# Norm of the latents issued under the last gate tile, with the latent attention's buffers laid out anew

## What is computed

```python
z = h @ w_in
qa, ka, va, cq, ckv, kpe, gate = jnp.split(z, ATT_SPLITS, axis=-1)
cq = _rmsnorm(cq, g_qa)
q_nope = jnp.einsum('bsc,chd->bshd', cq, w_uq)
q_pe = _rope(jnp.einsum('bsc,chr->bshr', cq, w_uqr), pos)
q_lat = jnp.einsum('bshd,chd->bshc', q_nope, w_uk)
ckv = _rmsnorm(ckv, g_kva)
kpe = _rope(kpe[:, :, None, :], pos)[:, :, 0, :]
# differential attention on qa, ka, va; latent attention on q_lat, q_pe, ckv, kpe
o = jnp.concatenate([o_a, o_b], axis=-1) * jax.nn.silu(gate)
return o @ w_out, new_rows
```

## Time and profile before

| | us |
|---|---|
| median of 3 runs | 2079.89 (2076.95 to 2081.9) |
| profiled execution | 2074.99 |
| its span | 2073.2 |
| TensorE busy | 1850.0 (89%) |
| VectorE busy | 1255.5 (61%) |
| ScalarE busy | 411.3 (20%) |
| GpSimd busy | 197.4 (10%) |
| mean granted TensorE clock | 0.945 |

### The profile page before, as it was taken

The page is one execution under the profiler, slowest core; times in us unless marked ns, Lnnn a source line. Parts: engine busy times, 40 slices in busy tenths (PEclk is TensorE's granted clock), DMA queues, the critical chain, the costliest instruction groups (busy, mean ns, idle before and its releaser), DMA issues.

```text
span 2073.2 us, 32711 instructions
## 1 busy us (share of the span) xinstructions
PE 1850.0 (89%) x13182; PEld 1699.9 (82%) x13182; DVE 1255.5 (61%) x1598; ACT 411.3 (20%) x912; POOL 197.4 (10%) x117
## 2 busy tenths in 40 slices
PE   5548999999999978997987899968999999999995
PEld 0108999999999966776876778957999999999995
DVE  4899667667867653554355544376777544584444
ACT  1241000000010012332355443431000000131111
POOL 2770000000600000000000011210000000001110
PEclk8879999999999999998889898989999999999997
DMA  9555555545655422216134244214444333452222
GB/s 388 226 223 192 205 191 212 193 189 193 238 205 209 182 102 62 62 32 178 60 113 138 84 143 173 91 61 158 180 182 187 126 108 120 163 194 86 81 81 86
DMA packets 86104, 316.04 MB, mean 152 GB/s; under 512 B 12184, under 2 KB 20552, under 8 KB 60448
## 3 DMA queue, kind: packets, MB, share of 16 engines
q1 hardware_dynamic: 64208, 237.70, 31.6%
q10 hardware_dynamic: 21200, 76.48, 10.3%
q0 software_dynamic: 640, 1.10, 0.1%
HBM read 282.56 MB, written 32.69 MB: 152 GB/s over the span
## 4 chain that ended last, share of the span: by engine, by line
PE 66%; DVE 14%; DMA 7%; issue 5%; ACT 5%; POOL 2%; SPq 0%; DVEq 0%; ACTq 0%; POOLq 0%
PE banks L718 66%; DVE banks L1604 3%; DMA w_raw<-in_w_pin 3%; POOL ssq L676 2%; DMA w_adr<-in_w_ada_dve 2%; DMA w_more<-in_w_ada_pe 1%; ACT pxd L1387 1%; DMA d_raw<-pool_d_scratch 1%; DVE w_hi L1566 1%; DVE std L1839 1%; DVE h_lo L395 1%; DVE rstd L1546 1%; DVE x L2034 1%; ACT px L1305 0%; DVE pt_lo L1773 0%
## 5 line engine op out<-in xcount | busy, mean ns | idle before, releaser
L718 PE MATMUL banks<-h_hi,w_hi 128*128 128x272 f32 x3968 | 830.2, 295 | 61.0 <-DVE w_lo L1567 29.5
L718 PE MATMUL banks<-h_lo,w_hi 128*128 128x272 f32 x3712 | 776.4, 291 | 0.0
L718 PE MATMUL banks<-h_hi,w_lo 128*128 128x272 f32 x3456 | 716.1, 289 | 0.0
L718 PEld LDWEIGHTS banks<-h_hi,w_hi 128*128 128x128 f32 x3968 | 630.6, 193 | 72.5 <-issue 45.9
L718 PEld LDWEIGHTS banks<-h_lo,w_hi 128*128 128x128 f32 x3712 | 594.1, 192 | 0.0
L718 PEld LDWEIGHTS banks<-h_hi,w_lo 128*128 128x128 f32 x3456 | 545.5, 190 | 0.0
L1604 DVE CUSTOM_DVE_ANT_0 banks<-w_adr,cond_b 128x2048 f32<-128x2048 f32 x160 | 386.2, 2414 | 19.0 <-DMA w_adr<-in_w_ada_dve 15.8
L1566 DVE CAST w_hi<-w_raw 128x2048 fp32r<-128x2048 f32 x101 | 125.6, 1244 | 219.7 <-PE banks L718 168.2
L1567 DVE TENSOR_TENSOR w_lo<-w_raw,w_hi 128x2048 fp32r<-128x2048 f32 x101 | 249.2, 2467 | 3.5
L1251 ACT ACTIVATE stage<-banks 128x544 f32<-128x544 f32 x48 | 30.1, 627 | 514.4 <-PE banks L718 514.4
L1927 DVE TENSOR_TENSOR x<-x,stage 128x544 f32 (+1 forms) x32 | 23.9, 748 | 168.3 <-ACT stage L1469 168.3
(11 more groups left out here) (293 smaller groups left out, 1696.6 us busy)
## 6 DMA issues: line engine op xcount, KB each, us to landing
w_adr<-in_w_ada_dve ACTq DMA_DIRECT2D x46, 1024.0 KB, 5.0
w_adr<-in_w_ada_dve SPq DMA_DIRECT2D x34, 1024.0 KB, 4.9
w_raw<-in_w_z SPq DMA_DIRECT2D x32, 1024.0 KB, 6.2
w_raw<-in_w_pin SPq DMA_DIRECT2D x32, 1024.0 KB, 6.0
w_raw<-in_w_gate SPq DMA_DIRECT2D x16, 1024.0 KB, 6.9
w_raw<-in_w_out SPq DMA_DIRECT2D x32, 512.0 KB, 3.8
w_raw<-in_w_pout SPq DMA_DIRECT2D x16, 1024.0 KB, 4.8
w_more<-in_w_ada_pe SPq DMA_DIRECT2D x10, 1024.0 KB, 7.4
```

The lines of the kernel that those rows point to most:

```text
L718: return pe.matmul(out, lhsT, rhs, start=start, stop=stop)
```

## The change

TensorE issues the `mq_sum` matmuls between gate tiles 14 and 15 (of 0 to 15), into banks 4 to 7. The swap matmuls follow tile 15. TensorE no longer waits for `kp_done` before item 0. VectorE evicts the sums and scales both latents at once, without waiting for the last tile; its waits on the last eviction and on `stored`, and the rotation of `kpe`, come behind the scaling. ScalarE takes the two square roots between the evictions of gate tiles 14 and 15, and waits for `stored` ahead of `kpe_hi`. SyncE waits for `adr_used` alone before the weights of head pair 0; its waits on `mm_done` and `stored` stand before `load_sg(0)`. The buffers are moved so that these writes don't meet anything in use. In the differential attention `vds` gets its own semaphore and stays early; `qds`, `kds` and the first `vcs` are now loaded after the sample stage (`ms_fin`, `latent_out`), ahead of the first loads of `x`. The diff, cut to its core (the other moved buffers have the same form):

```diff
+        vds = sb("vds", [P, HEADS, NS], scope=over_ptd)
@@ latent attention buffers
         fo = sb("fo", [P, NP], scope=ml_loop)
+        pt_hi = sb("pt_hi", [P, 2, QT, NP], F32R, ml_loop)
+        pt_lo = sb("pt_lo", [P, 2, QT, NP], F32R, ml_loop)
+        qs0 = sb("qs0", [P, 2, NP], F32R, ml_loop)
         wq = sb("wq", [P, 2, LT, P], scope=ml_loop)
...
+        sb("under_ckT", [P, LT * R], scope=early)
+        lat_r0 = sb("lat_r0", [P, R], scope=early)
+        lat_r1 = sb("lat_r1", [P, R], scope=early)
@@ sync
-            sp.wait_ge(mm_done, G_OUT)
             sp.wait_ge(adr_used, ADA_P0 + ADA_P1)
-            for s in range(2):
-                sp.wait_ge(stored[s], 16 * (ZT + GT) // 2)
...
                 if t == 0:
+                    sp.wait_ge(mm_done, G_OUT)
+                    for s in range(2):
+                        sp.wait_ge(stored[s], 16 * (ZT + GT) // 2)
                     load_sg(0)
...
-            for z0, dst in ((ZQ, qds), (ZK, kds), (ZV, vds)):
-                sp.dma_start(dst[:], z_out[z0:z0 + HEADS, :, NP:R].rearrange("h p r -> p h r")).then_inc(new_in, 16)
+            sp.dma_start(vds[:], z_out[ZV:ZV + HEADS, :, NP:R].rearrange("h p r -> p h r")).then_inc(vds_in, 16)
             load_cache(0)
-            load_vcache(0)
...
             sp.wait_ge(latent_out, 32)
+            for z0, dst in ((ZQ, qds), (ZK, kds)):
+                sp.dma_start(dst[:], z_out[z0:z0 + HEADS, :, NP:R].rearrange("h p r -> p h r")).then_inc(new_in, 16)
+            load_vcache(0)
@@ tensor
-            big_loop(G_GATE, 0, GT // 2)
-            for s in range(2):
-                pe.wait_ge(acc_free[s], turn_of(G_OUT + (G_OUT + s) % 2))
+            big_loop(G_GATE, 0, GT // 2 - 1)
+            big_wait(G_GATE + GT - 2)
+            big_tile((G_GATE + GT - 2) % 2)
             pe.wait_ge(lat_step, 2 * (2 * LT - 1))
             pe.wait_ge(adr_used, ADA_P0 + ADA_P1)
             for a in range(2):
                 for hf in range(2):
-                    m = small(PS[:, 2 * a + hf, 0:HALF], ones[:], lat_sum[:, a, hf * HALF:(hf + 1) * HALF], True, True)
+                    m = small(PS[:, 4 + 2 * a + hf, 0:HALF], ones[:], lat_sum[:, a, hf * HALF:(hf + 1) * HALF], True, True)
                 m.then_inc(mq_sum, 1)
+            big_wait(G_GATE + GT - 1)
+            big_tile((G_GATE + GT - 1) % 2)
+            pe.wait_ge(mq_var, 2)
             for a in range(2):
                 m = small(PS[:, 6 + a, 0:HALF], swap_t[:], kpe[:, a * HALF:(a + 1) * HALF], True, True)
             m.then_inc(kp_swap, 1)
+            for s in range(2):
+                pe.wait_ge(acc_free[s], turn_of(G_OUT + (G_OUT + s) % 2))
             pe.wait_ge(mq_var, 2)
             pe.wait_ge(mq_norm, 1)
-            pe.wait_ge(kp_done, 1)
...
-            pe.wait_ge(new_in, 48)
+            pe.wait_ge(vds_in, 16)
...
+                    pe.wait_ge(new_in, 32)
@@ scalar
+            last_gate(0)
             act.wait_ge(mq_in, 32)
             for a in range(2):
                 act.wait_ge(mq_var, a + 1)
                 act.activation(lat_r[a][:], lat_r[a][:], ACT.Sqrt).then_inc(mq_std, 1)
+            last_gate(1)
+            for s in range(2):
+                act.wait_ge(stored[s], 16 * (ZT + GT) // 2)
             act.wait_ge(kp_done, 1)
@@ vector
-            dve.wait_ge(mm_done, G_OUT)
-            for s in range(2):
-                dve.wait_ge(acc_free[s], turn_of(G_OUT + (G_OUT + s) % 2))
-            dve.wait_ge(stored[0], 16 * (ZT + GT) // 2)
-            dve.wait_ge(stored[1], 16 * (ZT + GT) // 2)
-            dve.memset(lam_in[:, 0, 0:1], 0.0).then_inc(qps_free, 1)
             for a in range(2):
                 dve.wait_ge(mq_sum, a + 1)
...
-            dve.wait_ge(kp_swap, 1)
-            dve.tensor_tensor(rows(qpr[:]), PS[:, 6:8, 0:HALF], rows(sin_t[:]), ALU.mult)
-            vchain(dve, dve.tensor_tensor(kpe[:], kpe[:], cos_t[:], ALU.mult))
-            dve.tensor_tensor(kpe[:], kpe[:], qpr[:], ALU.add).then_inc(kp_done, 1)
             for a, (lat, g_v) in enumerate(((cq, gqa_v), (ckT, gkva_v))):
...
                 ins.then_inc(mq_norm, 1)
+            dve.wait_ge(mq_norm, 2)
+            dve.memset(lam_in[:, 0, 0:1], 0.0).then_inc(qps_free, 1)
+            dve.wait_ge(mm_done, G_OUT)
+            for s in range(2):
+                dve.wait_ge(acc_free[s], turn_of(G_OUT + (G_OUT + s) % 2))
+            dve.wait_ge(stored[0], 16 * (ZT + GT) // 2)
+            dve.wait_ge(stored[1], 16 * (ZT + GT) // 2)
+            dve.wait_ge(kp_swap, 1)
+            dve.tensor_tensor(rows(qpr[:]), PS[:, 6:8, 0:HALF], rows(sin_t[:]), ALU.mult)
+            vchain(dve, dve.tensor_tensor(kpe[:], kpe[:], cos_t[:], ALU.mult))
+            dve.tensor_tensor(kpe[:], kpe[:], qpr[:], ALU.add).then_inc(kp_done, 1)
```

More of the change, by code:

```diff
@@ L236, in program @@
         qn_lo0 = sb("qn_lo0", [P, 2, R], F32R, ml_loop)
-        qs0 = sb("qs0", [P, 2, NP], F32R, ml_loop)
-        qn_s = sb("qn_s", [P, 2, NS], scope=ml_loop)
         qpe = sb("qpe", [P, R], scope=ml_loop)
         qsin = sb("qsin", [P, R], scope=ml_loop)
+        qn_s = sb("qn_s", [P, 2, NS], scope=ml_loop)
         st = sb("st", [P, 4, 4 * HEADS], scope=ml_loop)
-        pt_hi = sb("pt_hi", [P, 2, QT, NP], F32R, ml_loop)
-        pt_lo = sb("pt_lo", [P, 2, QT, NP], F32R, ml_loop)
         ml_loop.close()
+        mla.close()
         early = ExitStack()
-        sb("early_rest", [P, LT * R], scope=early)
+        sb("under_ckT", [P, LT * R], scope=early)
+        lat_r0 = sb("lat_r0", [P, R], scope=early)
+        lat_r1 = sb("lat_r1", [P, R], scope=early)
+        sb("under_cq", [P, (LT * HEADS + HEADS) * NS + 2 * R - 2 * R + LT * R], scope=early)
         lat_sum = sb("lat_sum", [P, 2, R], scope=early)
         lat_sq = sb("lat_sq", [P, R], scope=early)
-        sb("early_more", [P, 4 * NP + 2 * 2 * LT * P + LORA * 2 + LT * P + 2 * LT * P + 4 * R - 3 * R], scope=early)
-        lat_r0 = sb("lat_r0", [P, R], scope=early)
-        lat_r1 = sb("lat_r1", [P, R], scope=early)
         early.close()
@@ L282, in program @@
         sb("half_w", [P, 2 * D], scope=dif)
+        qd = sb("qd", [P, 2, NP], scope=dif)
+        kd = sb("kd", [P, 2, NP], scope=dif)
+        vd = sb("vd", [P, 2, NP], scope=dif)
+        kcs = sb("kcs", [P, 2, PAST], scope=dif)
+        qds = sb("qds", [P, HEADS, NS], scope=dif)
+        kds = sb("kds", [P, HEADS, NS], scope=dif)
+        vcs = sb("vcs", [P, 2, QT, P], scope=dif)
         qd_hi = sb("qd_hi", [P, 2, NP], F32R, dif)
@@ L287, in program @@
         pxds = sb("pxds", [P, SKEYS], scope=dif)
[L288 to L296, removed]
         ptds = sb("ptds", [P, KTS, 2, NS], scope=dif)
         ptd1 = sb("ptd1", [P, KTS, 2, NS], scope=dif)
-        sb("under_cond", [P, 1600], scope=dif)
+        sb("under_cond", [P, 2464], scope=dif)
         rs8 = sb("rs8", [HEADS, R], scope=dif)
@@ L1258, in _, with last_gate @@
             store_loop(G_GATE, 0, GT // 2 - 1, ACT.Silu, g2, 16 * ZT // 2, ADA_P0 + ZT)
-            store_loop(G_GATE, GT // 2 - 1, GT // 2, ACT.Silu, g2, 16 * ZT // 2)
+            def last_gate(s):
+                g = G_GATE + GT - 2 + s
+                act.wait_ge(mm_done, g + 1)
+                act.activation(rows(stage[:, s]), acc[g % 2], ACT.Silu).then_inc(acc_free[g % 2], 1)
+                act.wait_ge(acc_free[g % 2], turn_of(g + 2))
+                act.dma_start(g_scr[GT - 2 + s], stage[:, s]).then_inc(stored[s], 16)
+            last_gate(0)
             act.wait_ge(mq_in, 32)
```

8 lines of the change are left out of this document (4 added, 4 removed).

## The result

The changed kernel takes 2073.83 us (median of 13 runs, 2070.06 to 2075.99), the kernel before in the same comparison 2079.89 (13 runs, 2073.62 to 2081.9). The ratio is 0.9975, with a 95% interval of 0.9966 to 0.9985. So it is faster, by 5.2 us by the ratio and 6.1 by the medians, where 11.5 was predicted. The profiled execution took 2070.06, in a span of 2068.3 us (2073.2 before).

What follows compares the result with a forecast made beforehand. It took TensorE, busy from 200 to 740 us, then a chain of mostly VectorE waits about 752 us as the bound. Item 1 11.5 us earlier gave 2079.89 - 11.5 = 2068.4 us, range 2063 to 2077.

Steps and rivals of the forecast that it cites:

- the chain up to item 1: From the last gate tiles to head pair 0's second item: item 1 starts at 761.8, not 773.26, 11.5 us earlier.
- the 0.3 us to spare: At the kpe rotation: the norm ends at 756.6, the store lands at 756.9; any further delay counts in full.
- The early weights: Head pair 0's weights issued 18 us earlier, so item 0 isn't late; 3.4 of the 11.5 us hang on it.
- The later edits: Loads of qds, kds and first vcs after the sample stage: slack of at least 15 us, so cost nothing.
- (c): Latent attention, 773 to 965 us: more TensorE work at half clock, kernel slower at about 2085.5 us; chance 0.06.
- (d): Another wait holds item 1 or a later point, such as differential attention loads; gain below 4 us; chance 0.06.
- Rival (a): Before tile 15's eviction: an exposed table load makes the chain 1.28 us later, gain 10.2 us; chance 0.10.
- The further drain of 1.38 us: At ScalarE's root: the skill's extra cost per table switch, not added; with it the gain would be about 10.4 us.
- One loop iteration becomes straight code: TensorE's gate tiles: costed at nothing, or some tenths of a us for an instruction fetch at most.
- rival (b): Later work moved against TensorE's clock falls: 2.5 to 7.5 us of gain left, 2072.4 to 2077.4 us; chance 0.16.

Runs made afterwards that it cites:

- b2_unrolled_pair: Kernel before, with only TensorE's last two gate tiles written as straight code behind the loop; ratio to before 1.0023.
- b4_one_loop: Kernel before, with TensorE's z and gate loops joined to one, so one pair of tiles less code; ratio to before 1.0012.
- b7_pad: Kernel before, with 64 small matmuls, result unused, at the head of TensorE's program; ratio to before 1.0021.
- b1_late_sample_loads: Kernel before, with only the later edits: qds, kds and first vcs loaded after the sample stage, vds on its own semaphore; ratio to before 1.0009.
- b5_two_pairs: Kernel before, with the last pair of z tiles and the last pair of gate tiles as straight code; ratio to before 1.0002.
- b6_straight_at_end: Kernel before, with the last pair of the last output projection, at the kernel's end, as straight code; ratio to before 1.0004.
- a4_one_loop: Changed kernel, with TensorE's z and gate loops joined to one, so its program is as long as before; ratio to before 0.9962.
- a7_pad: Changed kernel, with 64 small matmuls, result unused, at the head of TensorE's program; ratio to before 0.9968.
- a0_after_again: Changed kernel run once more, unaltered; ratio to before 0.9969.
- a6_nops: Changed kernel, with 128 empty instructions at the head of TensorE, which don't seem to be in the program; ratio to before 0.9978.
- a3_item0_first: Changed kernel, with item 0 evicted by ScalarE ahead of its wait for the stores and two output issues; ratio to before 0.9952.
- a5_item0_first_one_loop: Changed kernel, with item 0 evicted first and the z and gate loops joined; ratio to before 0.9929, median 2064.9 us.
- the three copies: The changed kernel's first run, its unaltered rerun, and its run with empty instructions; ratios to before 0.9975, 0.9969 and 0.9978.
- a1_filler: Changed kernel, with seven idle matmuls, result unused, on TensorE between items 0 and 1; ratio to before 0.9987.

## Why the prediction missed the size

**What held.** The direction, and the chain up to item 1. Each of its terms stands in the timelines of after, against its own start: tile 15 evicted 13.86 us behind tile 14 (13.93 by the sum), end of the norm at 757.88, 16.6 behind tile 14's eviction (16.5), rotation from 758.19 to the issue of `kpe_out` at 760.44 2.25 us (2.14), from there to the eviction of item 0 1.23 (1.05), and from there to item 1 1.70 (1.70). Together 11.06 us instead of 11.5. The end of the norm and the landing of the store came within 0.1 us of each other: of the 0.3 us to spare in the sum nothing was left. The early weights are worth 3.3 us (3.4), but that the two agree is partly luck: without them item 1 starts 5.65 us later, since item 0 starts late and runs at low clock, and gives some of it back by running at full clock itself, none of which the sum had. The later edits cost nothing that shows. (c) did not come: the clock between 773 and 965 us is 0.97. (d) looked behind the edit too, but for loads of the differential attention, which is no longer than before (223.5 us, 223.9 before).

**Rival (a)** was wrong, as forecast: the SiLU table is loaded at 745.58, 9.5 us ahead of the last eviction. The root starts at 744.36, right where its table load of 1.28 us ends at 743.06 + 1.28 = 744.34. The further drain of 1.38 us that the Trainium skill gives (ScalarE: Activation LUTs, "What ACT_TABLE_LOAD costs") isn't in these rows any more than in those of before; the measurement decides. Had it been there, it would have counted in full, since the norm had nothing to spare.

**The step that failed** is "One loop iteration becomes straight code ... I cost it at nothing (... above, a fetch of instructions of some tenths of a us)". It was priced for the place at which the code stands, and there it is right: TensorE has no gap there. The cost arises 500 us later, in a stage the change doesn't touch. The straight pair is one and a half packets, and shifts the rest of TensorE's program by half a packet against the moments at which it is needed. What it is worth has three readings. Within the kernel before: mean ratio 1.0019 for b2_unrolled_pair, b4_one_loop and b7_pad, against 1.0005 for b1_late_sample_loads, b5_two_pairs and b6_straight_at_end: 0.0014 x 2080 = 2.9 us. Within the changed kernel: 0.9974 against 0.9965 (a4_one_loop and a7_pad), 1.9 us. With item 0 first: 0.9952 against 0.9929, 4.8 us. About 3 us in all, and not better known than to 2 us: the intervals overlap widely in the second reading and a little in the third, and in the first those of b2_unrolled_pair and b7_pad begin at 1.0012 and 1.0010 where those of b5_two_pairs and b6_straight_at_end end at 1.0013 and 1.0014. That the shift causes it is shown by b7_pad, which has no other edit that could. How it takes 3 us is shown in two pieces, both in the stage behind 1235 us: the half weights land after 7.0 us and not 5.9, with the packet in the queues' rows, and TensorE does the same matmuls in 4.2 us more (means of one profile per kernel, 772.0 to 776.5 us against 768.2 to 773.7), at half clock for more of the time. How these two hang together was not tested.

**The second term** is the clock, which rival (b) had, but at another place. The prediction took the fall before item 0 for something that the change removes ("The change closes the large gap"). It moved. Before, the clock was low during item 0, which isn't on the path: it ends at 764.80 + 5.58 = 770.38, ScalarE comes to it at 771.56, and item 1 starts 2.88 us behind its end. With the 1.73 us that lie between them at least, item 0 could be 6.7 us long at no cost. Now item 0 runs at full clock and the fall comes after it, at item 1, which is on the path: a mean of 5.67 us over after, a0_after_again, a4_one_loop, a6_nops and a7_pad, against 3.92 before, 1.8 us. That the gap is what does it is shown by a3_item0_first and a5_item0_first_one_loop, in which it is 1.73 us. The prediction had even worked out that item 0 would be done at 759.0 and evicted at 760.1; item 1 was to start at 761.8. That is a gap of 2.8 us on TensorE, and it never asked what the clock would do in it.

**The measured time** of 2073.83 us lies in the stated range, and in rival (b)'s part of it (2072.4 to 2077.4). That is partly luck: (b) has TensorE's work at half clock take 4 to 9 us of the gain, because the change moves that work. At item 1 it took 1.8. The rest comes of the shifted program and comes without the change as well, in b2_unrolled_pair and b7_pad, though much of it is work at half clock too.

**The balance.** 11.06 - 1.8 - 3 = 6.3 us, where 5.2 (by the ratio) and 6.1 (by the medians) were measured, 5.4 as the mean of the three copies' ratios. With 2 us of uncertainty in the 3 that is a weak check. The column "latent" agrees with its part: a mean of 394.9 for the seven kernels of before's order and 385.3 for the five of the changed order with early weights and no filler, 9.6 us, where 11.06 - 1.8 = 9.3. With item 0 first it is 382.2, or 12.8 us: the gap of 1.9 us goes as well, not the clock alone.

**What stays open:** why the clock falls more often behind 1235 us in the shifted kernels; why a4_one_loop kept its clock through 3.62 us; why a7_pad got back some 1 us and not 2 to 3 (in its profile TensorE is busy for 773.7 us of the last stage, the most of the 7 kernels without the shift, so its clock was low there although its load landed early).

## What to carry to other kernels

Here a chain moved under idle time could be summed to half a us; what lay beyond it needed its own look. When a gap on TensorE is closed, find the next gap and whether the work behind it is on the path: issue whatever fills or frees it first (evicting item 0 before two stores gave 0.9952 instead of 0.9974). And where the length of TensorE's code changes by a loop iteration or more, allow for the whole kernel to move by 0.1 to 0.2% for that alone, and look for it with a kernel that has the shift and nothing else, before explaining a small ratio by the edit.

## What the runs showed of the hardware that was not expected

- TensorE's program comes over the DMA engines in packets of 16 KB (36 of them, 0.59 MB). With one beside a load of half weights the load landed about 1.1 us later (5.68 to 6.00 us in 7 kernels, 6.81 to 7.17 in 9); the packet keeps one engine busy for about 1.0 us.
- The three kernels that are the one before with such a shift alone took 1.0012 to 1.0023 of its time, three others without the shift 1.0002 to 1.0009, and the loss lies in a stage 500 us behind the edit. It doesn't follow the amount of code: one pair less lands late, two pairs more land as early as none.
- In that stage the same 5891 matmuls kept TensorE busy for 768.2 to 776.5 us in the 16 profiles, by how long it was granted 1.2 GHz and not 2.4 (71.5 to 91.6 us).
- A gap of 3.6 us on TensorE let its clock fall from 2.4 to 1.2 GHz in 4 profiles of 5, one of 1.73 us in none of 2. 3.4 us of extra matmuls at full clock ahead of a gap of 2.4 us didn't prevent it (a1_filler).
- A store of the same size landed 4.4 us after its issue in a1_filler (756.82 to 761.21) and in 2.1 in the median of before.
